# Last norm of an encoder made inside its sixteenth expert, on the sums of fifteen

## What is computed

```python
x = x + expert_choice_ffn(rms_norm(x, norm_ffn[l]), router_w[l], router_b[l], exp_w_gate[l], exp_w_up[l], exp_w_down[l])
return rms_norm(x, norm_final)      # y = x * rsqrt(mean(x*x) + 1e-6) * norm_final, row by row
...
gate, idx = lax.top_k(aff.T, cap)   # each of 16 experts takes its top tokens: 64 of the prompt, 128 of the sample
xe = xf[idx]
hid = silu(xe @ w_gate) * (xe @ w_up)
ye = (hid @ w_down) * gate
y = zeros.at[idx].add(ye)
```

## Time and profile before

| what | us |
|---|---|
| median of 3 runs | 2710.6 (2709.3 to 2712.37) |
| the profiled execution, its own time | 2707.34 |
| its span in the profile | 2705.6 |
| last matmul ends | 2651.56 |
| last expert's adds seen landed by POOL | 2664.0 |
| `final_norm` issues its first load | 2670.2 |
| DVE ends the last tile | 2694.95 |

### The profile page before, as it was taken

How to read it: one execution, slowest core, us unless ns; L and a number is a source line. 1 busy time by engine, 2 the same in 40 slices (tenths; PEclk the granted TensorE clock), 3 DMA queues, 4 the chain that set the end, 5 groups by cost and what they waited for, 6 DMA issues and landing times. The chain is left out here.

```text
span 2705.6 us, 50239 instructions
## 1 busy us (share of the span) xinstructions
PE 2443.5 (90%) x19612; PEld 2062.2 (76%) x19612; DVE 1817.4 (67%) x2468; ACT 1205.4 (45%) x1753; POOL 704.2 (26%) x689
## 2 busy tenths in 40 slices
PE   6999999999976999995799996799999999999992
PEld 4777777777765999983566674689999988999991
DVE  5448868787764666554777677577767777777772
ACT  5444444444411333333334331555555565555552
POOL 3133233333302344442553533000011110011000
PEclk9999999999997999997899998799999999999996
DMA  3234242443444766644537352777777777777745
GB/s 133 69 112 139 87 152 74 133 132 94 140 165 135 197 185 185 181 120 132 170 119 253 110 187 101 288 250 247 241 221 251 240 241 246 249 231 235 248 152 206
DMA packets 294150, 476.87 MB, mean 176 GB/s; under 512 B 142049, under 2 KB 209777, under 8 KB 266337
## 3 DMA queue, kind: packets, MB, share of 16 engines
q1 hardware_dynamic: 280048, 428.25, 48.5%
q0 software_dynamic: 7680, 26.82, 4.9%
q10 hardware_dynamic: 6256, 19.47, 2.1%
HBM read 362.20 MB, written 110.69 MB: 175 GB/s over the span
## 5 line engine op out<-in xcount | busy, mean ns | idle before, releaser
L2502 PE MATMUL bank<-e_xt,e_w_high 128*128 128x384 f32 x1792 | 526.4, 357 | 1.3 <-DVE e_xt L2638 1.3
L2625 DVE TENSOR_TENSOR e_w_low<-e_w,e_w_high 128x2048 fp32r<-128x2048 f32 x192 | 436.5, 2288 | 95.8 <-ACT e_w_high L2558 95.8
L2503 PE MATMUL bank<-e_xt,e_w_low 128*128 128x192 f32 x1792 | 449.9, 251 | 0.0
L2558 ACT ACTIVATE e_w_high<-e_w 128x2048 fp32r<-128x2048 f32 x192 | 365.9, 1908 | 108.6 <-PE bank L2524 82.4
L2503 PEld LDWEIGHTS bank<-e_xt,e_w_low 128*128 128x128 f32 x1792 | 343.0, 191 | 0.6
L2502 PEld LDWEIGHTS bank<-e_xt,e_w_high 128*128 128x128 f32 x1792 | 338.9, 189 | 3.4 <-issue 1.6
L463 PE MATMUL bank<-h_high,w_high 128*128 128x512 f32 x864 | 264.1, 414 | 0.3 <-DVE work L864 0.3
L466 PE MATMUL bank<-h_low,w_high 128*128 128x512 f32 x864 | 246.5, 393 | 0.0
L469 PE MATMUL bank<-h_high,w_low 128*128 128x512 f32 x864 | 244.9, 392 | 0.0
L2448 POOL DMA_INDIRECT xacc_dram<-e_y,e_put x32 | 50.8, 1588 | 735.5 <-DVE e_y L2660 730.7
L847 DVE SCALAR_TENSOR_TENSOR work<-work,vec 128x1551 f32<-128x1551 f32 x116 | 216.1, 1863 | 2.4
(11 more groups left out here) (313 smaller groups left out, 5347.3 us busy)
## 6 DMA issues: line engine op xcount, KB each, us to landing
e_w<-in_ew SPq DMA_DIRECT2D x192, 1024.0 KB, 5.7
features_dram<-work SPq DMA_DIRECT2D x48, 512.0 KB, 3.8
fe<-features_dram SPq DMA_DIRECT2D x24, 1024.0 KB, 6.0
x_w<-in_w_mix SPq DMA_DIRECT2D x48, 512.0 KB, 3.7
w<-in_w_in SPq DMA_DIRECT2D x38, 512.0 KB, 5.2
ba_tok_dram<-work SPq DMA_DIRECT2D x96, 128.0 KB, 2.3
gates_dram<-work ACTq DMA_DIRECT2D x16, 768.0 KB, 4.6
all<-ba_tok_dram SPq DMA_DIRECT2D x96, 128.0 KB, 3.2
```

The costliest lines, as they stand in the source:

```text
L2502: nc.tensor.matmul(*wide, start=(k == 0), stop=False)
L2503: nc.tensor.matmul(*narrow, start=False, stop=False)
L2558: nc.scalar.activation(w_high[n % RING][:], w[n % RING][:], ACT.Copy).then_inc(w_high_done, 1)
L2625: tt(w_low[n % RING][:], w[n % RING][:], w_high[n % RING][:].bitcast(F32), ALU.subtract)\
```

## The change

- `final_norm` and its block are gone. Its buffers too: a tile is now held in half of a weight slot, `x_out[t]` = half t%2 of `w[t//2]`.
- SP issues the load of the norm's weights as the first transfer of `experts`, ahead of all weight loads.
- After its last weight load SP waits for the adds of expert 14 (`added`, 15 * 32) and, for each pair of tiles, for the split of the unit that last used the slot. It loads tiles 0 to 11 of `xacc` and then stores each tile to `out` when it is normed. At the end it waits for all stores and for two row transfers (`put_out`).
- ACT squares tiles 0 and 1 in the last expert's steps f = 5 and 6, tile 2 after the last silu, takes the roots of three tiles at a time, and squares tiles 3 to 11 after the last `hidden_high`, ahead of `fold_low`.
- DVE normalises tiles 0 to 8 ahead of its wait for the last matmul, then merges the expert's 192 rows: `ye` = bank * gate + the row read back. Then it normalises tiles 9 to 11 and last the 192 rows.
- POOL gathers the expert's 192 rows of `xacc` (sums through expert 14) into `xe`, waits until all twelve tiles are stored, and writes the 192 normed rows over those in `out` by two indirect transfers that don't accumulate. The last expert's two adds are gone.

```diff
@@ -2417,6 +2417,17 @@
             sem(f"e_{n}") for n in ("down_done", "scaled", "added", "weights_ready", "folded", "joined"))
         FT = FF // P
+        NT, LAST = T // P, E - 1
+        x_out = [w[t // 2][:, (t % 2) * D:(t % 2 + 1) * D] for t in range(NT)]
+        norm, junk = sb("e_norm", [P, D]), sb("e_junk", [P, D])
+        stats = sb("e_stats", [P, NT + 2, 4])
+        x_in, norm_in, gathered, stored, put_out = (
+            [sem(f"e_x_in{t}") for t in range(NT)], sem("e_norm_in"), sem("e_gathered"), sem("e_stored"), sem("e_put_out"))
+        squared, rooted, inverted, normed = (sem(f"e_{n}") for n in ("squared", "rooted", "inverted", "normed"))
+        merged, row_squared, row_rooted, row_inverted, row_normed = (
+            sem(f"e_{n}") for n in ("merged", "row_squared", "row_rooted", "row_inverted", "row_normed"))
         def upcoming(e, n):
             return (e, n) if n < UNITS else (e + 1, n - UNITS)
@@ -2430,7 +2441,20 @@
                             apart(sp, g, w_split, e * UNITS + (n - RING + 1))
                         sp.dma_start(w[n % RING][:], a["ew"][e, n, :, :]).then_inc(w_in[n % RING], 16)
+                sp.dma_start(norm[:], a["norms"][1:2, :].to_broadcast([P, D])).then_inc(norm_in, 16)
                 repeat(sp, E, load)
+                sp.wait_ge(added, LAST * 32)
+                for t in range(NT):
+                    if t % 2 == 0:
+                        sp.wait_ge(w_split, LAST * UNITS + RING + t // 2 + 1)
+                    sp.dma_start(x_out[t], g.xacc[t * P:(t + 1) * P, :]).then_inc(x_in[t], 16)
+                for t in range(NT):
+                    sp.wait_ge(normed, t + 1)
+                    sp.dma_start(a["out"][t * P:(t + 1) * P, :], x_out[t]).then_inc(stored, 16)
+                sp.wait_ge(stored, 16 * NT)
+                sp.wait_ge(put_out, 32)
             @block.gpsimd
             def _(pool):
@@ -2449,11 +2473,23 @@
                                                 None, compute_op=ALU.add).then_inc(added, 16)
                     apart(pool, g, added, e * 32 + 32)
+                def rows_out():
+                    pool.wait_ge(turned, 4 * E)
+                    for n in range(2):
+                        pool.indirect_dma_start(xe[n][:], None, g.xacc, bass.IndirectOffsetOnAxis(ap=row[n][:], axis=0))\
+                          .then_inc(gathered, 16)
+                    pool.wait_ge(stored, 16 * NT)
+                    for n in (1, 0):
+                        pool.wait_ge(row_normed, 2 - n)
+                        pool.indirect_dma_start(a["out"], bass.IndirectOffsetOnAxis(ap=row[n][:], axis=0), ye[n][:], None)\
+                          .then_inc(put_out, 16)
                 fetch(0)
                 with pool.Fori(0, E - 1) as e:
                     fetch(e + 1)
                     add(e)
-                add(E - 1)
+                rows_out()
             @block.tensor
             def _(pe):
@@ -2575,6 +2611,26 @@
                                                    g.bank[half][CAP[0]:2 * CAP[0], :], ACT.Copy)
                     ins.then_inc(folded, 1)
+                def square(t):
+                    act.wait_ge(x_in[t], 16)
+                    if t:
+                        act.wait_ge(squared, t)
+                    nc.scalar.activation(junk[:], x_out[t], ACT.Square, accum_out=stats[:, t, 0:1]).then_inc(squared, 1)
+                def root(lo, hi):
+                    act.wait_ge(squared, hi)
+                    nc.scalar.activation(stats[:, lo:hi, 1], stats[:, lo:hi, 0], ACT.Sqrt, bias=g.c("eps", 0, 1),
+                                         scale=1.0 / D).then_inc(rooted, 1)
+                def row_root(n):
+                    act.wait_ge(merged, 4 - 2 * n)
+                    act.wait_ge(squared, NT)
+                    r, t = slice(0, CAP[n]), NT + n
+                    nc.scalar.activation(junk[r, :], ye[n][:], ACT.Square, accum_out=stats[r, t, 0:1]).then_inc(row_squared, 1)
+                    act.wait_ge(row_squared, 2 - n)
+                    nc.scalar.activation(stats[r, t, 1:2], stats[r, t, 0:1], ACT.Sqrt, bias=g.c("eps", 0, 1, rows=r),
+                                         scale=1.0 / D).then_inc(row_rooted, 1)
                 def expert(e, more=True):
                     for f in range(FT):
                         act.wait_ge(up_done, e * FT + (f + 1))
@@ -2591,7 +2647,17 @@
                         nc.scalar.activation(act_[f % 2][:], sums[f % 2][:, 0, :], ACT.Silu).then_inc(silu_done, 1)
                         if f >= 1 and (more or f + 5 < UNITS):
                             weights_high(*upcoming(e, f + 5))
+                        if not more and f in (5, 6):
+                            square(f - 5)
+                    if not more:
+                        square(2)
+                        root(0, 3)
                     hidden_high(e, FT - 1)
+                    if not more:
+                        for lo in (3, 6, 9):
+                            for t in range(lo, lo + 3):
+                                square(t)
+                            root(lo, lo + 3)
                     if more:
                         tokens_high(e + 1, 0)
                         tokens_high(e + 1, 1)
@@ -2601,6 +2667,9 @@
                         for n in range(2, RING):
                             weights_high(e + 1, n)
                     fold_low(e)
+                    if not more:
+                        row_root(1)
+                        row_root(0)
                 for n in range(2):
                     weights_high(0, n)
@@ -2658,6 +2727,54 @@
                     for half in range(2):
                         c = slice(half * BLK, (half + 1) * BLK)
                         nc.vector.tensor_scalar(ye[0][:, c], ye[0][:, c], wt[0][:], None, ALU.mult).then_inc(scaled, 1)
+                def normalise(t):
+                    if t % 3 == 0:
+                        dve.wait_ge(rooted, t // 3 + 1)
+                        nc.vector.reciprocal(stats[:, t:t + 3, 2], stats[:, t:t + 3, 1]).then_inc(inverted, 1)
+                        dve.wait_ge(inverted, t // 3 + 1)
+                    nc.vector.scalar_tensor_tensor(x_out[t], x_out[t], stats[:, t, 2:3], norm[:], ALU.mult, ALU.mult)\
+                        .then_inc(normed, 1)
+                def merge(n):
+                    dve.wait_ge(gathered, 32)
+                    for half in range(2):
+                        c = slice(half * BLK, (half + 1) * BLK)
+                        src = g.bank[2 + half][:] if n else ye[0][:, c]
+                        nc.vector.scalar_tensor_tensor(ye[n][:, c], src, wt[n][:], xe[n][:, c], ALU.mult, ALU.add)\
+                            .then_inc(merged, 1)
+                def row_normalise(n):
+                    r, t = slice(0, CAP[n]), NT + n
+                    dve.wait_ge(row_rooted, 2 - n)
+                    nc.vector.reciprocal(stats[r, t, 2:3], stats[r, t, 1:2]).then_inc(row_inverted, 1)
+                    dve.wait_ge(row_inverted, 2 - n)
+                    nc.vector.scalar_tensor_tensor(ye[n][:], ye[n][:], stats[r, t, 2:3], norm[r, :], ALU.mult, ALU.mult)\
+                        .then_inc(row_normed, 1)
+                def finish(e):
+                    dve.wait_ge(added, e * 32)
+                    for n in range(2):
+                        ins = nc.vector.tensor_copy(wt[n][:], g.gate[0:CAP[n], n, bass.ds(e, 1)])
+                    ins.then_inc(weights_ready, 1)
+                    dve.wait_ge(norm_in, 16)
+                    for t in range(9):
+                        normalise(t)
+                    dve.wait_ge(weights_ready, e + 1)
+                    dve.wait_ge(down_done, e * FT + FT)
+                    merge(1)
+                    dve.wait_ge(folded, e + 1)
+                    for half in range(2):
+                        c = slice(half * BLK, (half + 1) * BLK)
+                        tt(ye[0][:, c], g.bank[half][0:CAP[0], :], fold[:, c], ALU.add).then_inc(joined, 1)
+                    dve.wait_ge(joined, e * 2 + 2)
+                    merge(0)
+                    for t in range(9, NT):
+                        normalise(t)
+                    row_normalise(1)
+                    row_normalise(0)
                 def expert(e, more=True):
                     if more:
@@ -2686,7 +2803,10 @@
                         tokens_low(e + 1, 3)
                         for n in range(2, RING):
                             weights_low(e + 1, n)
-                    scale(e)
+                    if more:
+                        scale(e)
+                    else:
+                        finish(e)
                 rows(0)
                 for n in range(2):
@@ -2696,55 +2816,6 @@
                 for n in range(2, RING):
                     weights_low(0, n)
                 repeat(dve, E, expert, lambda e: expert(e, False))
-
-
-def final_norm(nc, a, g):
...
         run(experts)
-        run(final_norm)
```

## The result

| | us | |
|---|---|---|
| before, median of 4 | 2709.99 | 2709.3 to 2712.37 |
| changed, median of 4 | 2673.86 | 2671.22 to 2676.5 |
| ratio | 0.9865 | 95% interval 0.9848 to 0.9882 |

The forecast was 2678.0 with a range of 2674.5 to 2683.5. The direction and the mechanism held, but the time fell 4.1 us under the forecast and 0.6 us under the range's lower end, so the range was wrong.

A forecast was written before the change was run, and what follows sets the result against it. The 54.0 us after PE's last matmul (adds, POOL's drain, `final_norm`) were taken as the bound; 34.5 + 6.2 - 8.1 = 32.6 us less gave 2710.6 - 32.6 = 2678.0, range 2674.5 to 2683.5.

The forecast's parts named there:

- two row transfers: POOL's indirect writes of the rows at the end: 7.4 us to seen landed, between gathers' 6.2 and adds' 8.55.
- Rival A: Block's end: POOL's drain comes wholly after the landing, adding 4.1 us, 2682.1; chance 0.11.
- B: Tail: the last stores land late, 10.5 us for 3.6, adding 6.9, 2684.9; chance 0.05.
- D: Last expert: norm isn't hidden, squares wait until after `fold_low`, 11.2 us later, 2689.2; chance 0.04.
- E: Last expert: first tile read back lands very late, PE stops before `down` step 6; 2711 or more; chance 0.03.
- Fourth root: ACT under the last expert: groups of squares and roots end at 2649.8, 1.8 us ahead of `fold_low`.
- DVE's spare time: DVE ahead of the last matmul: nine tiles take 11.7 us, to 2650.7, with 1 us left.
- The load in front: Start of the experts: norm weights first on SP's queue, 0.5 MB or 1.4 us, covered, cost 0.
- rival C: Start of the experts: gather or first units 1.4 us later, 2679.4, or 2681.6 with a full landing; chance 0.05.
- The part up to the last store's issue: Tail from the last matmul: merges to 2655.6, then tiles 9 to 11 take 4.0 us, to 2659.6.
- The last store's landing: Tail: the last store finds an almost empty queue and lands in 3.6 us, at 2663.2; bound above 10.5.
- The drain: Block's end: POOL drains from 2666.8; the longer of landing and 5.3 us from its start, to 2672.1.

The follow-up runs named there:

- e4_wait_drain: POOL waits for its two row transfers to land before its block's end, against the changed kernel: span 2672.5 us, tail 22.4 in place of 19.7.
- e8_no_rows: The two row transfers at the end left out, against the changed kernel; POOL still waits for all stores: span 2673.8 us, tail 17.2.
- e7_norm_late: Load of the norm's weights moved behind all weight loads on SP's queue, against the changed kernel: 2672.55 us median, ratio 0.9852, tail 19.7.
- e3_no_last_add: The last expert's two adds left out, against the kernel before: 2696.33 us median, ratio 0.9948, tail 39.9.
- e2_unhidden: All twelve squares, roots and products put behind the last matmul, against the changed kernel: 2686.31 us median, ratio 0.9913, tail 33.6.

## Why the mechanism held, and which steps of the prediction failed

- **What failed** is the size of two terms at the end of the tail, in the prediction's words the "two row transfers" (7.4 us, between 6.2 and 8.55; measured 4.8) and the last store ahead of them (3.9 us from DVE's last tile to the first row transfer; measured 3.1). They made the tail 1.7 us too long, worked out below. By estimate the forecast with the measured tail is 2678.0 - 1.7 = 2676.3, and the same range laid about it would begin at 2672.8 and hold the measured 2673.86.
- **The mechanism** held: squares of tiles 0 and 1 in the gaps of steps 5 and 6, nine tiles ahead of the merges, no stop of PE, granted clock 1.00 to the end, last transfers where they were expected. Rivals A, B, D and E did not occur.
- **ACT and DVE under PE.** Fourth root 2.3 us before the fold (forecast 1.8), DVE's spare time 1.95 (forecast 1).
- **The load in front**, taken as 0, costs about 0.3 us, where rival C had 1.4. The rule of the Trainium skill weighed there ("DMA: Bandwidth & Descriptors", Queues, rings and completion order: turns between queues, packet by packet) fits this better than strict order of issue does, though no run here puts the two side by side.
- **The part up to the last store's issue**: forecast 2659.6 - 2651.56 = 8.0 us after the last matmul. DVE ends tile 11 at 2659.28 + 3.68 = 2662.96, 7.9 after. Right.
- **The last store's landing**: taken as 3.6, the least in the earlier trace rows and a load's, bound above 10.5. The last three stores landed in 2.6 to 2.8 us; the first row transfer starts 3.1 us after DVE's last tile, where I had 3.9. Mis-sized by 0.8 us.
- **Two row transfers**: taken as 7.4 us between 6.2 and 8.55. Measured 2670.9 - 2666.06 = 4.8, under both bounds. This is the term that was most mis-sized, with its floor. Adds were a poor model: the same 0.79 MB kept the 16 DMA engines busy for 60.8% of 9.2 us = 5.6 us as the last two adds, and for 47.2% of 5.5 us = 2.6 us as plain row writes. Why the gathers of the earlier trace rows, the floor, took longer than 4.8 is open; they could share the DMA engines with weight loads, but no run separates this. Of the 2.6 us between 7.4 and 4.8 only 1.1 counts, since not the landing but the drain sets the end: both issues take 2668.25 - 2666.06 = 2.2 us (0.98 and 0.91 each), where the adds' 1.42 and 1.56 gave 3.3.
- **The drain**: taken as 5.3 us from its start, behind the second issue. Measured 2673.7 - 2668.25 = 5.45. `e4_wait_drain` and `e8_no_rows` show it with and without fresh transfers: 5.44 and 5.28. Rival A (a drain wholly after the landing) is refuted: the drain ends 2.8 us after it.
- **The sum**: 0.8 of the store and 1.1 of the issues make 1.9, of which 0.2 is given back by the drain: 1.7, and 21.4 - 19.7 = 1.7. The tail was 1.7 us too long.
- **The rest of the miss**, 4.1 - 1.7 = 2.4 us, is not in the tail. Of it 0.6 is that the kernel before, at 2710.6 in the forecast, gave 2709.99 beside the change. By the tail alone the change gives 2710.0 - 34.3 = 2675.7, inside the range; the medians gave 2673.86, 2671.45 and, of a near copy (`e7_norm_late`), 2672.55. The experts took 943.6 us in the profile after and 944.1 before, which explains 0.5 us at most, and the interval of the ratio is 4.6 us to either side. The phases ahead, which the change leaves alone, end anywhere within 8.9 us in the ten profiles. So the 1.8 us that are left need no cause in the change, but whether a small gain ahead of the tail exists stays open. What was wrong in the range is that its lower end left nothing for the spread of the untouched phases: I had three runs within 3 us of each other, and 11 runs span 18.6.

Where the 34.3 us came from: 14.2 were the adds and the drain that waited behind them (`e3_no_last_add`), 13.9 is what hiding the arithmetic is worth (`e2_unhidden`). That the two add up is assumed: the first was taken out of the kernel before, the second out of the change. The remaining 6.2 were not measured by themselves; they should be what is left of loads and stores that no longer follow each other, less what the new end costs: 2.5 us for the row transfers and 5.3 for a drain that did not go away, only its place changed.

## What to carry to other kernels

- A last phase that reads what the last step writes can be done on everything but the last step's part, if few rows are touched: here the two transfers of 192 of 1536 rows cost 2.5 us, and the tail is 34 us shorter.
- A block's end is work too: look for the drain of the engine that issues indirect transfers, and let that engine reach it early. Where its transfers land within some 5 us, its cost counts from that engine's last instruction, and a wait for the landing ahead of it only adds.
- When a total spreads by 0.3% and more, measure the changed part from a fixed event of the same execution (here the last matmul); it repeated within 0.1 us.

## What the runs showed of the hardware that I had not expected

- POOL's drain at the end of a block that had indirect transfers takes 5.1 to 5.4 us where nothing is left in flight, whether the transfers landed just before (5.28, 5.44 in `e4_wait_drain`, 5.11 in `e3_no_last_add`) or the last was issued some 45 us earlier (5.28 in `e8_no_rows`). In the change, with its transfers in flight, it ends 5.45 us after the second issue. In `final_norm` of before it ended with a later landing, after 7.5 us.
- It is not so at every block. Ahead of the experts, in the kernel before, POOL's last product ends at 2.34 + 1682.75 = 1685.09 and the drain 0.5 us later (1682.7 + 2.87). That block's POOL transfers were direct ones, issued by 1248.4. Whether the kind of transfer or its age makes the difference, and what the drain does in this time, no row shows.
- Two plain indirect writes of together 192 rows landed 4.8 us after the first was started, the accumulating ones took 8.55, with issues of 0.9 to 1.0 us against 1.4 to 1.6.
